# A hybrid decoder step on one core: state products in two tiles side by side, a minimum ahead of other work, another expert group kept on chip, and a closing stage with fewer VectorE products

## The chip, the cores and the metric

The kernel runs on one core of a Trainium2 chip. The metric is the device time of one execution in microseconds (us); lower is better. The engines of the core are called PE (TensorE), DVE (VectorE), ACT (ScalarE), POOL (GpSimd) and SP (SyncE, which here only issues DMAs). Each runs its own list of instructions in order and waits on semaphores.

## The reference, cut to what matters

One layer of a decoder, for 512 prompt tokens and 32 sample tokens (8 sequences of 4), `D_MODEL` 1024:

```
xn = rmsnorm(h); z, xbc, dt, gate, xl = split(xn @ w_in)
y_ssd = rmsnorm((ssd_chunked(conv(xbc), dt) + d_skip * xs) * silu(z))      # 16 heads of 64, state 64, chunks of 128
y_lru = rmsnorm(lru_scan(conv(xl)) * gelu(gate))
h = h + concat(y_ssd, y_lru) @ w_out
h = h + peer(rmsnorm(h))                    # 16384 experts of one neuron: act = gelu(t @ U), out = (gate * act) @ V
g = sigmoid(rmsnorm(h) @ w_ple_gate)
h = h + rmsnorm((p @ w_ple_proj) * g)
return rmsnorm(h), new states
```

For each of the 8 sample sequences the SSD part computes an output from the old state (`C . s0`) and a new state (`decay * s0 + B^T . (w * x)`). All is fp32.

## The kernel before, in words

Tensors lie feature-major: 8 blocks of 128 features on the partitions, 544 tokens along the free axis; the closing stage works on the two halves of 272 tokens (`q`). A precise product is made of three fp32r matmuls (high by high, high by low, low by high), so each weight block is first rounded on ScalarE (`Whi`, `Rh`) and its rest taken on VectorE (`Wlo`, `Rl`). The order on each engine is written out by hand, step by step in `n`; nothing is scheduled automatically.

**Mixer** (steps `n` 0 to 50, one weight tile of 48 matmuls each on TensorE). From step 35 on the tiles of the output projection are interleaved with the four chunks of the SSD scan. For chunk `c`, `l_min(c)` on VectorE limits the exponent (`L[c]`, 128x2048), `exps(c)` on ScalarE takes 16 exponentials of it, `scores(c)` on VectorE multiplies it by `CBm`; then `y_sum`, `state_in` (four products `xdt`, `xw`), `lru_add` (two additions over 544 tokens) and `lo` (the next `Wlo`). TensorE does `state`, `outputs`, `xs_tokens` and then its weight tile. After the chunks come the sample tokens: `sample_tokens` (turned to rows), `sample_outputs` (16 small products, and for each of 8 sequences a matmul of `CZ`, 128x64, with the old state `s0s`, 128x512, all added up in partitions 0 to 63 of one PSUM bank), `yoS` and `sample_turn` (turned back), `ssd_lo` (the low part `yl`), the sums of squares `sq8`, and from step 43 the last eight tiles with `sample_state(b)`: a matmul of `BTb`, 64x128, with `xwS`, 64x512, into bank 4 or 5.

**Experts.** 144 items through a ring of four slots (`Rw` by DMA, `Rh` ACT, `Rl` DVE): 16 query tiles, and 128 U blocks of 24 matmuls each over 384 tokens. Their activations go to memory (`acts`), gate values too (`gates`). Then 128 V items of 24 matmuls. V works in groups of four blocks: `load_a` brings the activations back to one of five buffers `Aq`, `load_g` two groups of gates to `Gq`, `h_full` (DVE) multiplies them, `h_hi` (ACT) rounds, `h_lo` (DVE) takes the rest, which the group's first item waits for. `VGRP` is the order of the groups; the last U group (31) is kept on chip and is third. The experts of the other 160 tokens go through POOL's gathers (`ug`, 512 KB each), with one VectorE operation per gathered row.

**Closing.** 16 gate products (`gate(i)`, half `i // 8`, block `i % 8`) on TensorE; DVE `scaled`, ACT `sigmoid`, DVE `gated`, ACT `gated_square`, DVE `square_add`; a total over features on TensorE, root on ACT, reciprocal on DVE; then `residual` (a gain and a factor, then the addition to `h`), squares of `h`, the last root, and `final` (gain and factor), from which SP stores `y` in 16 pieces.

Of the kernel before, what the change touches and what calls it, by code (L numbers as in the profile page):

```python
# [14 lines left out]
P = 128  # L15
# [28 lines left out]
VGRP = [0, 1] + list(range(PK // 4 - KEEP, PK // 4)) + list(range(2, PK // 4 - KEEP))  # L44
# [135 lines left out]
def mixer(nc, sh, ring, x, wm, par, head, w_rg, w_ig, conv_in, s0, lru0, ssd_p, ssd_s, conv_o, lru_o):  # L180
# [8 lines left out]
    def after(offset, size):  # L189
# [19 lines left out]
        ("segm", [64, NB], F32), ("smS", [64, 3, HG], F32), ("eS", [64, HG], F32), ("selJ", [NH, HG], F32),  # L209
# [26 lines left out]
        ("Ls", [64, HG, 32], F32), ("xdS", [64, HG * HD], F32), ("yoS", [64, HG * HD], F32),  # L236
# [6 lines left out]
    (xwS, ces), _ = plan(nc, LA + 16384, ("xwS", [64, HG * HD], F32), ("ces", [P, HG, 32], F32))  # L243
# [3 lines left out]
        ("stt", [P, HG * HD], F32), ("BTb", [64, NB, P], F32))  # L247
# [30 lines left out]
    def sync(sp):  # L278
# [21 lines left out]
        for n in range(2, NW):  # L300
# [11 lines left out]
            if n == 4:  # L312
                sp.wait_ge(S("const"), 28)
# [51 lines left out]
    def pool(g):  # L365
# [33 lines left out]
        g.wait_ge(k, 23)  # L399
# [8 lines left out]
        g.wait_ge(k, 28)  # L408
# [33 lines left out]
    def tensor(pe):  # L442
# [115 lines left out]
        def outputs(c):  # L558
            pe.wait_ge(S("scs"), c + 1)
            pe.wait_ge(S("xdw"), 4 * (c + 1))  # L560
            if c == 0:
                pe.wait_ge(S("cbm"), 2)
# [21 lines left out]
        def sample_tokens():  # L584
            pe.wait_ge(S("zc"), 5)
            pe.wait_ge(S("xdw"), 4 * NC)
            for jj in range(4):
                for g in range(NG):
                    m = pe.matmul(PS[0:64, 7, jj * P:(jj + 1) * P], XZ[:, 4 * g + jj, :], ident[:, :],
                                  start=(g == 0), stop=(g == NG - 1))  # L590
            m.then_inc(S("tr"), 1)

        def sample_outputs():
# [11 lines left out]
            for b in range(NB):  # L605
                m = pe.matmul(PS[0:64, 6, :].rearrange("p (j d) -> p j d", j=HG), CZ[:, b * 64:(b + 1) * 64],
                              s0s[:, :, b, :], start=(b == 0), stop=(b == NB - 1))
            m.then_inc(S("ymm"), 1)

        def sample_turn():  # L610
            pe.wait_ge(S("sad"), 1)
            for jj in range(4):
                m = pe.transpose(PS[:, 7, jj * 64:(jj + 1) * 64], yoS[:, jj * P:(jj + 1) * P], ident[0:64, 0:64])
            m.then_inc(S("ymm"), 1)

        def sample_state(b):
            pe.wait_ge(S("xdw"), 4 * NC + 2)
            pe.wait_ge(S("cbm"), 4)
# [3 lines left out]
            pe.matmul(PS[:, 4 + b % 2, :], BTb[:, b, :], xwS[:, :], start=True, stop=True).then_inc(S("stm"), 1)  # L622
# [59 lines left out]
    def scalar(a):  # L682
# [90 lines left out]
        for n in range(1, NW + 1):  # L773
# [50 lines left out]
            if n == 19:  # L824
# [7 lines left out]
                a.copy(smS[:, :, :], PS[0:64, 5, 0:3 * HG].rearrange("p (q j) -> p q j", q=3)).then_inc(S("tmv"), 1)  # L832
# [73 lines left out]
    def vector(v):  # L906
# [120 lines left out]
        def scores(c):  # L1027
            v.wait_ge(S("lexp"), c + 1)
            v.wait_ge(S("cbm"), 2)
# [113 lines left out]
        for n in range(1, NW + 1):  # L1143
# [10 lines left out]
            if n == 37:  # L1154
# [4 lines left out]
                state_in(1)  # L1159
            if n == 38:  # L1160
# [4 lines left out]
                state_in(2)  # L1165
            if n == 39:
# [9 lines left out]
            if n == 40:  # L1176
                v.wait_ge(S("tr"), 2 * NC + 1)
                src = PS[0:64, 7, :].rearrange("p (j d) -> p j d", j=HG)
                for dst, q in ((xdS, 1), (xwS, 2)):
                    v.tensor_tensor(dst[:, :].rearrange("p (j d) -> p j d", j=HG), src,  # L1180
                                    smS[:, q, :].unsqueeze(2).broadcast_to([64, HG, HD]), ALU.mult
# [10 lines left out]
            if n == 37:  # L1192
                l_min(2)
            if n == 38:
                l_min(3)
# [42 lines left out]
            if n == 8:  # L1238
# [3 lines left out]
                v.wait_ge(S("const"), 28)  # L1242
# [9 lines left out]
            if n == 10:  # L1252
# [3 lines left out]
                v.wait_ge(S("const"), 28)  # L1256
# [1306 lines left out]
```

## Time and profile before

| | |
|---|---|
| runs (3) | median 1787.02 us, 1786.6 to 1788.82 |
| the profiled execution | 1784.59 us |
| its span | 1782.6 us |
| PE busy | 1729.5 us, 97% |
| DVE busy | 1513.1 us, 85% |
| ACT busy | 836.7 us, 47% |
| POOL busy | 548.8 us, 31% |
| mean granted TensorE clock | 0.995 |

The span is what the profiler sees between first and last instruction; the 2 us beyond it belong to start and end. A matmul counts as busy until its modelled end, so neighbours overlap and PE's share is no measure of its efficiency. What counts is where an engine is idle and what ended that.

### The profile page before, as it was taken

Reading aid. Unit: us, or ns where it says so; the run is one execution under the profiler, and the core shown is the slowest. Engines: PE = TensorE matmul, PEld = TensorE weight load, DVE = VectorE, ACT = ScalarE, POOL = GpSimd, SP = SyncE. Lnnn points to the kernel's source line nnn. Section 1 sums busy time; section 2 is a strip of 40 time slices with the busy share of each in tenths; the row PEclk is TensorE's granted clock in tenths of the full one; section 3 lists DMA queues with packets and bytes.
Section 4 is the critical chain, followed back from the end, with each engine's and each line's share of the span. In section 5 each row is a group of like instructions: output and inputs, shape, how many; then the busy total and the mean of one; then the engine's idle time right before and its main releaser. Section 6 shows DMA issues by size and latency. Waiting matters only on the chain.

```text
span 1782.6 us, 29695 instructions
## 1 busy us (share of the span) xinstructions
PE 1729.5 (97%) x11346; PEld 1695.0 (95%) x11346; DVE 1513.1 (85%) x2744; ACT 836.7 (47%) x1206; POOL 548.8 (31%) x416
## 2 busy tenths in 40 slices
PE   7999997999999999999999999999999999999996
PEld 6999997889999999999999999999999999999995
DVE  7757998877678789999999999779888988899877
ACT  5556652443333233357777777423333323333163
POOL 3100220000000013345444444355555554556300
PEclk9999999999999999999999999999999999999998
DMA  4212342135335556789999999999999999999611
GB/s 161 92 64 80 136 143 101 65 133 186 117 130 171 176 169 232 264 309 352 380 362 368 344 355 379 397 389 398 396 396 397 396 398 397 396 394 388 226 60 51
DMA packets 164716, 461.12 MB, mean 259 GB/s; under 512 B 17152, under 2 KB 77632, under 8 KB 161888
## 3 DMA queue, kind: packets, MB, share of 16 engines
q1 hardware_dynamic: 118496, 291.43, 45.3%
q0 software_dynamic: 46080, 167.79, 25.1%
q8 instruction: 91, 1.49, 0.3%
q14 instruction: 49, 0.40, 0.1%
HBM read 404.61 MB, written 54.56 MB: 258 GB/s over the span
## 4 chain that ended last, share of the span: by engine, by line
PE 59%; DMA 21%; DVE 14%; ACT 3%; issue 3%; SPq 0%; POOL 0%; DVEq 0%; ACTq 0%
DMA Rw<-vn 16%; PE PS L478 12%; PE PS L1619 8%; PE PS L1620 8%; PE PS L1621 8%; PE PS L1602 5%; PE PS L1690 5%; DVE Rl L176 2%; PE PS L2251 2%; DMA ug<-vn,idxU 2%; PE PS L1632 2%; PE PS L1633 2%; PE PS L1634 2%; DVE ug L2040 1%; ACT Rh L171 1%
## 5 line engine op out<-in xcount | busy, mean ns | idle before, releaser
L171 ACT CAST Rh<-Rw 128x1024 fp32r<-128x1024 f32 x272 | 284.3, 1046 | 341.7 <-DMA Rw<-vn 299.7
L176 DVE TENSOR_TENSOR Rl<-Rw,Rh 128x1024 fp32r<-128x1024 f32 x272 | 332.6, 1223 | 101.6 <-ACT Rh L171 99.6
L1578 POOL DMA_INDIRECT ug<-un,idxU x160 | 240.5, 1503 | 524.6 <-DVE dots L2040 343.2
L1632 PE MATMUL PS<-Hh,Rh 128*128 128x384 f32 x1024 | 344.4, 336 | 8.1 <-DVE Hl L2032 4.7
L1619 PE MATMUL PS<-Xh,Rh 128*128 128x384 f32 x992 | 342.6, 345 | 3.8 <-DVE Rl L176 2.8
L1634 PE MATMUL PS<-Hh,Rl 128*128 128x384 f32 x1024 | 342.7, 335 | 0.0
L1633 PE MATMUL PS<-Hl,Rh 128*128 128x384 f32 x1024 | 342.7, 335 | 0.0
L1620 PE MATMUL PS<-Xl,Rh 128*128 128x384 f32 x992 | 334.2, 337 | 0.0
L1621 PE MATMUL PS<-Xh,Rl 128*128 128x384 f32 x992 | 333.3, 336 | 0.0
L1578 POOL DMA_INDIRECT ug<-vn,idxU x160 | 261.8, 1636 | 217.5 <-DVE yacc L2045 173.8
L1632 PEld LDWEIGHTS PS<-Hh,Rh 128*128 128x128 f32 x1024 | 192.7, 188 | 11.8 <-issue 6.5
L1633 PEld LDWEIGHTS PS<-Hl,Rh 128*128 128x128 f32 x1024 | 192.7, 188 | 0.0
L1634 PEld LDWEIGHTS PS<-Hh,Rl 128*128 128x128 f32 x1024 | 192.6, 188 | 0.0
L1619 PEld LDWEIGHTS PS<-Xh,Rh 128*128 128x128 f32 x992 | 186.6, 188 | 5.8 <-DVE Rl L176 4.6
L1620 PEld LDWEIGHTS PS<-Xl,Rh 128*128 128x128 f32 x992 | 186.6, 188 | 0.0
L1621 PEld LDWEIGHTS PS<-Xh,Rl 128*128 128x128 f32 x992 | 186.2, 188 | 0.0
L2045 DVE SCALAR_TENSOR_TENSOR yacc<-ug,coef,yacc 128x1024 f32<-128x1024 f32 x128 | 164.1, 1282 | 10.7 <-DMA ug<-vn,idxU 7.9
L1736 ACT ACTIVATE Ab<-PS 128x384 f32<-128x384 f32 x120 | 59.0, 491 | 238.8 <-PE PS L1621 235.9
L2040 DVE CUSTOM_DVE_ANT_0 ug<-ug,xtok 128x1024 f32<-128x1024 f32 x128 | 154.4, 1224 | 16.7 <-DMA ug<-un,idxU 16.2
L478 PE MATMUL PS<-xhi,Whi 128*128 128x272 f32 (+1 forms) x560 | 119.0, 294 | 9.9 <-DVE xlo L927 8.3
L478 PE MATMUL PS<-xhi,Wlo 128*128 128x272 f32 (+1 forms) x560 | 116.4, 289 | 0.0
L478 PE MATMUL PS<-xlo,Whi 128*128 128x272 f32 (+1 forms) x560 | 116.1, 289 | 0.0
(441 smaller groups left out, 3049.3 us busy)
## 6 DMA issues: line engine op xcount, KB each, us to landing
Rw<-uw SPq DMA_DIRECT2D x144, 512.0 KB
Rw<-vn SPq DMA_DIRECT2D x128, 512.0 KB
Wr<-wm SPq DMA_DIRECT2D x51, 512.0 KB, 3.3
gates<-stg SPq DMA_DIRECT2D x12, 2048.0 KB
acts<-Ab SPq DMA_DIRECT2D x124, 192.0 KB
Aq<-acts SPq DMA_DIRECT2D x31, 768.0 KB, 17.2
Gq<-gates SPq DMA_DIRECT2D x29, 768.0 KB
L<-acsd SPq DMA_DIRECT2D x4, 1024.0 KB, 7.2
```

The costliest lines, as they stand in the source:

```text
L171: a.copy(self.Rh[:, q, :], self.Rw[:, q, :]).then_inc(self.S("rhi"), 1)
L176: v.tensor_tensor(self.Rl[:, q, :], self.Rw[:, q, :], self.Rh[:, q, :].bitcast(F32), ALU.subtract).then_inc(self.S("rlo"), 1)
L478: r = pe.matmul(pair(b, m)[:, q, :], w_sb[:, s, k, 0:m], x_sb[:, k, q * HT:(q + 1) * HT], start=first, stop=last)
L1578: p.indirect_dma_start(out=ug[:, r % 4, :], out_offset=None, in_=un if r < IDC else vn, in_offset=bass.IndirectOffsetOnAxis(ap=idxU[:, r % ...
L1619: pe.matmul(out, Rh[:, q, w], x_hi[:, k, P:NP], start=(k == 0), stop=False)
L1620: pe.matmul(out, Rh[:, q, w], x_lo[:, k, P:NP], start=False, stop=False)
L1621: r = pe.matmul(out, Rl[:, q, w], x_hi[:, k, P:NP], start=False, stop=(k == ND - 1))
L1632: pe.matmul(out, Rh[:, q, w], hh, start=(g == 0), stop=False)
L1633: pe.matmul(out, Rh[:, q, w], hl, start=False, stop=False)
L1634: r = pe.matmul(out, Rl[:, q, w], hh, start=False, stop=(g == PK - 1))
L2040: v.tensor_tensor_reduce(ug[:, q, :], ug[:, q, :], (xtok if own else xtokS)[:, :], 1.0, 0.0, ALU.mult, ALU.add, dots[:, c:c + 1]).then_inc ...
L2045: v.scalar_tensor_tensor(out=y[:, :], in0=ug[:, q, :], scalar=coef[:, c:c + 1], in1=y[:, :], op0=ALU.mult, op1=ALU.add).then_inc(S("sdt"), 1)
```

## The change

What it does, part by part:

- **Mixer, tiles.** `sample_outputs` writes even sequences to partitions 0 to 63 and odd ones to 64 to 127 of the bank (two column tiles); `eS`, `yoS` and the other scalars have 128 partitions, and `sample_turn` adds the two halves by a product with `BZ`, which then holds the identity twice. `sample_state(b)` takes partitions 0 to 63 or 64 to 127 of `BTb` and `xwS` (two row tiles). To fill both halves, `token_scalars`, `sample_cb` and `sample_tokens` make their products twice, for each column half. POOL prepares four more small masks.
- **Mixer, order.** `l_min(2)` and `l_min(3)` stand directly behind `state_in` instead of behind `lru_add` and `lo`.
- **Experts.** `VGRP` is 0, 31, 1, 2, ...: the kept group is second. Group 1 is loaded five items into V instead of before it. `h_full(1)` and `h_hi(1)` come one and one item later.
- **Closing.** The gain of the residual and of the last norm is applied by ScalarE (`gain`, `final_gain`); VectorE multiplies and adds two blocks at a time (128x2x272), with plain two-operand products. The total of the first half, its reciprocal and its residuals come one gate earlier.

```diff
-VGRP = [0, 1] + list(range(PK // 4 - KEEP, PK // 4)) + list(range(2, PK // 4 - KEEP))
+VGRP = [0] + list(range(PK // 4 - KEEP, PK // 4)) + list(range(1, PK // 4 - KEEP))
...
             for jj in range(4):
                 for g in range(NG):
-                    m = pe.matmul(PS[0:64, 7, jj * P:(jj + 1) * P], XZ[:, 4 * g + jj, :], ident[:, :],
-                                  start=(g == 0), stop=(g == NG - 1))
+                    for u in range(2):
+                        m = pe.matmul(PS[64 * u:64 * u + 64, 7, jj * P:(jj + 1) * P], XZ[:, 4 * g + jj, :], ident[:, :],
+                                      start=(g == 0), stop=(g == NG - 1))
...
             for b in range(NB):
-                m = pe.matmul(PS[0:64, 6, :].rearrange("p (j d) -> p j d", j=HG), CZ[:, b * 64:(b + 1) * 64],
-                              s0s[:, :, b, :], start=(b == 0), stop=(b == NB - 1))
+                u = b % 2
+                m = pe.matmul(PS[64 * u:64 * u + 64, 6, :].rearrange("p (j d) -> p j d", j=HG),
+                              CZ[:, b * 64:(b + 1) * 64], s0s[:, :, b, :], start=(b < 2), stop=(b >= NB - 2))
...
-                m = pe.transpose(PS[:, 7, jj * 64:(jj + 1) * 64], yoS[:, jj * P:(jj + 1) * P], ident[0:64, 0:64])
+                m = pe.matmul(PS[:, 7, jj * 64:(jj + 1) * 64], yoS[:, jj * P:(jj + 1) * P], BZ[:, :],
+                              start=True, stop=True)
...
-            pe.matmul(PS[:, 4 + b % 2, :], BTb[:, b, :], xwS[:, :], start=True, stop=True).then_inc(S("stm"), 1)
+            r = slice(64 * (b % 2), 64 * (b % 2) + 64)
+            pe.matmul(PS[:, 4 + b % 2, :], BTb[r, b, :], xwS[r, :], start=True, stop=True).then_inc(S("stm"), 1)
...
                 state_in(1)
+                l_min(2)
...
-            if n == 37:
-                l_min(2)
...
-            if n == GEND:
+            g = m - VI
+            if g == 5:
                 sp.wait_ge(S("gmm"), NU)
-                load_a(1)
-            g = m - VI
+                load_a(2)
...
-        def residual(q, k):
-            v.scalar_tensor_tensor(out=half(mv[:, k, :], q), in0=half(mv[:, k, :], q), scalar=sh.col("norm_plo", k),
-                                   in1=rstdO[:, q, :], op0=ALU.mult, op1=ALU.mult).then_inc(S("csc"), 1)
-            v.wait_ge(S("csc"), q * ND + k + 1)
-            v.tensor_tensor(half(h[:, k, :], q), half(h[:, k, :], q), half(mv[:, k, :], q), ALU.add
-                            ).then_inc(S("res"), 1)
+        def residual(q, p):
+            v.wait_ge(S("csm"), q * ND + 2 * p + 2)
+            v.tensor_tensor(two(mv, q, p), two(mv, q, p), over_two(rstdO[:, q, :]), ALU.mult).then_inc(S("csc"), 1)
+            v.wait_ge(S("csc"), q * (ND // 2) + p + 1)
+            v.tensor_tensor(two(h, q, p), two(h, q, p), two(mv, q, p), ALU.add).then_inc(S("res"), 2)
```

The first place is VectorE in step 37 of the mixer, from the last product of `state_in(1)` to the exponent of chunk 2 (`L_159`); before:

```order
L1039 TENSOR_TENSOR xw<-PS,TM 128x512
L1087 TENSOR_TENSOR tmpL<-PS,rstdL 128x544 [waits ole,rst,mm]
L1089 TENSOR_TENSOR h<-h,tmpL 128x544 [waits ole]
L912 TENSOR_TENSOR Wlo<-Wr,Whi 128x1024 [waits whi]
L1016 TENSOR_TENSOR L_159<-L_159,TM 128x2048 [waits tmv,ab1]
L1053 TENSOR_TENSOR stt<-ST,dec 128x512 [waits stu,cem]
L1057 TENSOR_TENSOR ST<-stt,PS 128x512 [waits stm,stu]
L1061 COPY dec<-ce 128x8 [waits ce1]
L1063 TENSOR_TENSOR ce<-ce,xs 128x1024 [waits cem]
L1031 TENSOR_TENSOR L_159<-L_159,CBm 128x2048 [waits cbm,lexp]
```

and with the change:

```order
L1055 TENSOR_TENSOR xw<-PS,TM 128x512
L1032 TENSOR_TENSOR L_159<-L_159,TM 128x2048 [waits tmv,ab1]
L1103 TENSOR_TENSOR tmpL<-PS,rstdL 128x544 [waits ole,rst,mm]
L1105 TENSOR_TENSOR h<-h,tmpL 128x544 [waits ole]
L928 TENSOR_TENSOR Wlo<-Wr,Whi 128x1024 [waits whi]
L1069 TENSOR_TENSOR stt<-ST,dec 128x512 [waits stu,cem]
L1073 TENSOR_TENSOR ST<-stt,PS 128x512 [waits stm,stu]
L1077 COPY dec<-ce 128x8 [waits ce1]
L1079 TENSOR_TENSOR ce<-ce,xs 128x1024 [waits cem]
L1047 TENSOR_TENSOR L_159<-L_159,CBm 128x2048 [waits cbm,lexp]
```

The minimum moved ahead of two additions and one weight split; the product that waits for the exponentials (`lexp`) stands where it stood.

The second place is SP's queue around the last U items and the first V items (`Rw<-vn` is a V block into the ring); before:

```order
L164 DMA Rw<-vn 128x1024 [waits rlo,rhi]
L1505 DMA Aq_227<-acts 128x4x384 [waits as2,as1,as3,as0,gmm]
L164 DMA Rw<-vn 128x1024 [waits rlo,rhi] x3
L1514 DMA Gq_239<-gates 128x6x128 [waits gw1]
L1514 DMA Gq_239<-gates 128x6x128
L164 DMA Rw<-vn 128x1024 [waits rlo,rhi]
L1514 DMA Gq_239<-gates 128x6x128 x2
```

and with the change:

```order
L164 DMA Rw<-vn 128x1024 [waits rlo,rhi] x3
L1520 DMA Aq_228<-acts 128x4x384 [waits as2,as1,as3,as0,gmm]
L164 DMA Rw<-vn 128x1024 [waits rlo,rhi]
L1533 DMA Gq_239<-gates 128x6x256 [waits gw1]
L164 DMA Rw<-vn 128x1024 [waits rlo,rhi]
L1533 DMA Gq_239<-gates 128x6x256
```

The activations of the second V group are gone from here; those of the third are loaded two ring blocks further on. The gate pieces of 128 numbers now belong to `Gq_238`, earlier in the queue.

The third place is VectorE at the end, from the reciprocal of the second half's first norm on; before (eight pairs like the first two, of which six are left out at the dots):

```order
L2374 RECIPROCAL c_rstdO<-c_rstdO 128x272 [waits root]
L2399 SCALAR_TENSOR_TENSOR c_mv<-c_mv,par,c_rstdO 128x272 [waits rst]
L2402 TENSOR_TENSOR h<-h,c_mv 128x272 [waits csc]
L2399 SCALAR_TENSOR_TENSOR c_mv<-c_mv,par,c_rstdO 128x272
L2402 TENSOR_TENSOR h<-h,c_mv 128x272 [waits csc]
...
L2374 RECIPROCAL c_rstdF<-c_rstdF 128x272 [waits root]
L2408 SCALAR_TENSOR_TENSOR c_y<-h,par,c_rstdF 128x272 [waits rst]
L2408 SCALAR_TENSOR_TENSOR c_y<-h,par,c_rstdF 128x272 x7
```

and with the change (four pairs, two left out):

```order
L2416 RECIPROCAL c_rstdO<-c_rstdO 128x272 [waits root]
L2448 TENSOR_TENSOR c_mv<-c_mv,c_rstdO 128x2x272 [waits csm,rst]
L2450 TENSOR_TENSOR h<-h,c_mv 128x2x272 [waits csc]
L2448 TENSOR_TENSOR c_mv<-c_mv,c_rstdO 128x2x272 [waits csm]
L2450 TENSOR_TENSOR h<-h,c_mv 128x2x272 [waits csc]
...
L2416 RECIPROCAL c_rstdF<-c_rstdF 128x272 [waits root]
L2456 TENSOR_TENSOR c_y<-c_y,c_rstdF 128x2x272 [waits csm,rst]
L2456 TENSOR_TENSOR c_y<-c_y,c_rstdF 128x2x272 [waits csm] x3
```

Half as many operations stand there, each over two blocks, and they wait for ScalarE's gains (`csm`).

## Rows read from the trace of the kernel before

**Rows 1.** Windows: stretch, us, busy per engine, granted clock, DMA share, GB/s.

```profile
250.00:310.00 60.00, 48.97 (x502) 44.20 (x501) 52.10 (x79) 26.28 (x73) 0.52 (x2) 0.97 0.46 145
...
1131.00:1603.00 472.00, 464.00 (x2652) 460.52 (x2650) 408.33 (x344) 156.69 (x144) 244.10 (x153) 1.00 1.04 395
...
1743.00:1782.60 39.60, 22.32 (x132) 17.52 (x130) 33.65 (x68) 14.31 (x33) 0.00 (x0) 0.88 0.17 57
```

**Rows 2.** Timeline, VectorE, mixer: start, us, operation, [idle before <- who ended it].

```profile
273.36 2.28 DVE L1016 TENSOR_TENSOR L<-L,TM 128x2048 f32<-128x2048 f32 x1
...
280.49 2.29 DVE L1031 TENSOR_TENSOR L<-L,CBm 128x2048 f32<-128x2048 f32 x1 [2.18 <-ACT L L754]
...
296.83 2.29 DVE L1031 TENSOR_TENSOR L<-L,CBm 128x2048 f32<-128x2048 f32 x1 [2.19 <-ACT L L754]
...
319.71 0.72 DVE L1087 TENSOR_TENSOR tmpL<-PS,rstdL 128x544 f32<-128x544 f32 x1
320.46 0.73 DVE L1089 TENSOR_TENSOR h<-h,tmpL 128x544 f32<-128x544 f32 x1
321.10 1.22 DVE L912 TENSOR_TENSOR Wlo<-Wr,Whi 128x1024 fp32r<-128x1024 f32 x1
323.60 0.68 DVE L1329 TENSOR_TENSOR yoS<-PS,eS 64x512 f32<-64x512 f32 x1 [1.28 <-PE PS L606]
...
335.94 1.40 DVE L1113 SCALAR_TENSOR_TENSOR yl<-xs,par,yh 128x32 fp32r<-128x32 f32 x8 [2.25 <-ACT sq L886]
```

**Rows 3.** Timeline, ScalarE: the exponentials of chunk 2.

```profile
275.67 4.78 ACT L754 ACTIVATE L<-L,nacm 128x128 f32<-128x128 f32 x16 [10.61 <-DVE L L1016]
```

**Rows 4.** Timeline, TensorE, mixer: small products and where it waits.

```profile
220.31 1.16 PE L527 MATMUL PS<-xs 64*128 64x128 f32 x16
...
303.73 1.08 PE L554 MATMUL PS<-xw,Btok 128*64 128x512 f32 x4 [3.22 <-DVE xw L1039]
304.61 1.95 PE L571 MATMUL PS<-L,xdt 128*64 128x128 f32 x32
...
307.52 1.96 PE L589 MATMUL PS<-ident,XZ 128*64 128x128 f32 x16
...
316.48 7.08 PE L606 MATMUL PS<-s0s,CZ 128*64 128x512 f32 x16
...
344.71 1.15 PE L670 MATMUL PS<-sq,ones 128*128 128x272 f32 x4 [0.20 <-DVE sq L1358]
...
358.13 1.98 PE L622 MATMUL PS<-xwS,BTb 64*128 64x512 f32 x4
```

**Rows 5.** Windows, behind a wait of TensorE in the mixer.

```profile
278.00:281.00 3.00, 3.00 (x15) 3.00 (x14) 0.82 (x2) 3.00 (x10) 0.00 (x0) 0.50 0.59 178
```

**Rows 6.** Timelines, VectorE and TensorE, first V group.

```profile
1144.56 1.23 DVE L2040 CUSTOM_DVE_ANT_0 ug<-ug,xtok 128x1024 f32<-128x1024 f32 x1 [1.75 <-DMA ug<-un,idxU]
...
1151.61 1.76 DVE L2025 TENSOR_TENSOR Aq<-Aq,Gq 128x1536 f32<-128x1536 f32 x1 [3.01 <-DMA Aq<-acts]
...
1148.75 0.66 PE L1632 MATMUL PS<-Hh,Rh 128*128 128x384 f32 x1 [3.04 <-DVE Hl L2032]
```

**Rows 7.** Chain of waits: start, us, what; two gate products of the closing.

```profile
1737.12 6.03 PE PS L2251 x48
```

**Rows 8.** Timelines, VectorE and then SP, end of the closing.

```profile
1743.17 0.44 DVE L2381 TENSOR_TENSOR c_tmp<-PS,c_rstdG 128x272 f32<-128x272 f32 x1 [1.27 <-PE PS L2251]
...
1756.39 0.43 DVE L2381 TENSOR_TENSOR c_tmp<-PS,c_rstdG 128x272 f32<-128x272 f32 x1
...
1760.39 1.85 DVE L2374 RECIPROCAL c_rstdO<-c_rstdO 128x272 f32<-128x272 f32 x1 [1.36 <-ACT c_rstdO L2306]
...
1769.39 1.84 DVE L2374 RECIPROCAL c_rstdF<-c_rstdF 128x272 f32<-128x272 f32 x1
...
1776.46 3.39 DVE L2408 SCALAR_TENSOR_TENSOR c_y<-h,par,c_rstdF 128x272 f32<-128x272 f32 x8
...
1776.99 3.79 SPq L2214 DMA_DIRECT2D y<-c_y  x8
```

More of the change, by code:

```diff
@@ L1165, in vector @@
                 state_in(2)
+                l_min(3)
             if n == 39:
@@ L1435, in experts @@
     GRP = 4 * 4 * DT
-    a_at = [R0 + 8 * GRP, R0, R0 + 2 * GRP, R0 + 7 * GRP, ring.end]
+    a_at = [R0 + 8 * GRP, R0 + 2 * GRP, R0, R0 + 7 * GRP, ring.end]
     Aq = [nc.alloc_sbuf_tensor_at("Aq%d" % q, [P, 4, DT], F32, offset=o) for q, o in enumerate(a_at)]
@@ L2101, in vector @@
                 h_lo(g // 4 + 1)
-            if g >= -2 and g % 4 == 2 and g // 4 + 2 < PK // 4:
+            if g == -1:
+                h_full(1)
+            if g >= 2 and g % 4 == 2 and g // 4 + 2 < PK // 4:
                 h_full(g // 4 + 2)
@@ L2302, in gated_square, with gain, final_gain @@
             a.activation(sq[:, i % 4, :], half(mv[:, n, :], q), ACT.Square).then_inc(S("csq"), 1)
+        def gain(i):
+            q, n = i // ND, i % ND
+            a.wait_ge(S("csq"), ND + i + 1)
+            a.activation(half(mv[:, n, :], q), half(mv[:, n, :], q), ACT.Copy, scale=sh.col("norm_plo", n)
+                         ).then_inc(S("csm"), 1)
+        def final_gain(q, k):
+            a.wait_ge(S("res"), q * ND + k + 1)
+            a.activation(half(yb[:, k, :], q), half(h[:, k, :], q), ACT.Copy, scale=sh.col("norm_fin", k)
+                         ).then_inc(S("csm"), 1)
         def root(buf, src, count):
@@ L2354, in scalar @@
                 a.preload_act_table(ACT.Sigmoid)
-            if i >= 12:
-                for k in range(2 * (i - 12), 2 * (i - 12) + 2):
+            elif i >= 1:
+                gated_square(i - 1)
+                gain(i - 1)
+            if i >= 11 and i < 15:
+                for k in range(2 * (i - 11), 2 * (i - 11) + 2):
                     res_square(0, k)
@@ L2360, in scalar @@
         root(rstdO[:, 1, :], PS[:, 7, 0:HT], 8)
+        gain(2 * ND - 1)
         root(rstdF[:, 0, :], PS[:, 6, 0:HT], 11)
         for k in range(ND):
-            res_square(1, k)
+            final_gain(0, k)
+            if k % 2 == 1 and k >= 3:
+                res_square(1, k - 3)
+                res_square(1, k - 2)
+        res_square(1, ND - 2)
+        res_square(1, ND - 1)
         root(rstdF[:, 1, :], PS[:, 7, 0:HT], 11 + ND)
+        for k in range(ND):
+            final_gain(1, k)
     def vector(v):
@@ L2446, in vector @@
         recip(rstdO[:, 1, :], 7)
-        for k in range(ND):
-            residual(1, k)
+        for p in range(ND // 2):
+            residual(1, p)
         final(0)
```

142 lines of the change are left out of this document (81 added, 61 removed).

## The prediction

> **What bounds the kernel now.** I read the windows first, to find stretches in which TensorE is idle, then the timelines of the engine it waits for. Over the 472 us from 1131 on TensorE is busy for 464.0; between 250 and 310 us it is busy for 49.0 of 60, and from 1743 on for 22.3 of 39.6 [rows 1]. So three places have something to give, and they are the three that the change touches; elsewhere only TensorE's own work counts.
>
> *Mixer, 250 to 310.* VectorE is the pacemaker. It waits twice for ScalarE's exponentials, 2.18 and 2.19 us [rows 2], and ScalarE in turn had been idle for 10.61 us before them because the minimum came so late [rows 3]. TensorE waits 3.22 us for VectorE's `xw` [rows 4]. From 310 to 345 TensorE has no gap, but it is only just covered: at 344.71 it still waits 0.20 us for the sums of squares, the end of a VectorE and ScalarE chain that begins at `yoS`, 323.60 [rows 2, 4]. Whatever TensorE saves in between is worth no more than that chain gains.
>
> *First V group.* TensorE waits 3.04 us for `Hl`; shortly before VectorE had waited 1.75 us for a gathered row, and behind `Hl` it waits 3.01 us for the activations of group 1 [rows 6]. But the DMA engines run at a share of 1.04 and 395 GB/s over the whole of 1131 to 1603 [rows 1].
>
> *Closing, from 1743.* VectorE. Two gate products take 6.03 us on TensorE [rows 7], 3.01 each. The eleventh gate's factor followed its product at once (1743.17, after a wait of 1.27), so the last one, four gates on, could have been at 1755.2; it stands at 1756.39 [rows 8]. Then follow the reciprocal at 1760.39, residuals to 1769.39, and two finals.
>
> **Mixer, order of the minimum.** `l_min` is put ahead of two additions and a split. From start to start these take 0.75 (319.71 to 320.46), 0.64 (to 321.10) and about 1.14 us [rows 2], 2.5 together, more than each wait. ScalarE was idle, so both waits go: 2.18 + 2.19 = **4.4 us**. What is late in exchange: the two additions and `Wlo`, by the 2.28 us of the minimum [rows 2]. `Wlo` is for the next weight tile, ahead of which TensorE does the state products and sits in its 11 us of idle time [rows 1]; cover enough. If that cover were gone it would cost up to 2.28 per step.
>
> **Mixer, column tiles.** `sample_outputs` takes 7.08 us for 8 products of 128x64 with 128x512 [rows 4]. `state` is the same shape, with its two products already in the two column halves: the next operation starts 0.88 us after them (303.73 to 304.61) [rows 4]. So 8 products come to 4 x 0.88 = 3.5 us, 3.5 less. Of these only a part reaches the chain: `yoS` waited for TensorE, but before that VectorE was busy with a split until 1.28 us earlier [rows 2], so `yoS` can move by 1.3 beyond the 4.4. The chain gains 4.4 + 1.3 = **5.7 us** at 344.71. It has no slack I can see elsewhere: TensorE's wait of 0.20 says that TensorE, which gains 4.4 + 3.5 = 7.9, will arrive early and wait about 2 us, at the first tile that needs `yl` (335.94) or at 344.71.
>
> The doubled products for the other half: `sample_tokens` has 16 records in 1.96 us and gets 32, alternating between the halves; `outputs` does 32 of the same 128 moving columns, alternating, in 1.95 [rows 4]. So nothing is added. The Trainium skill ("TensorE: Matmul & The Clock Gate", "Part 3: Packing small matmuls — row/col tiling") says that a weight load overlaps running products only when its row group differs; column tiles share their row group. By that rule the doubling would show in full, 1.96 us on the chain, and the sum below would be 9.8 instead of 11.8. The row of `outputs` speaks against it, and I go by the row.
>
> **Mixer, row tiles.** `sample_state`: two products take 1.98 us one after the other [rows 4]. The trace has no 512-column product in two row tiles. Bounds: nothing gained, or the 0.88 to 1.08 us of the column pair, 0.9 to 1.0 gained. The nearest row is `cb`, 16 records of 64x128 with 128 columns, alternating rows, in 1.16 us, 0.07 each, against 0.12 each for the 16 records of `sample_tokens` in one tile [rows 4]: row tiles do run side by side. I take 0.95 for each of four pairs. The first pair stands before the wait at 344.71 and is hidden in it; three count: **2.9 us**. After 350 nothing but TensorE's own work sets the pace there.
>
> **Mixer, additions.** Three tiny products in `token_scalars`, one in `sample_cb`, four longer ones in `sample_turn`: by the 0.07 to 0.12 us of small records [rows 4] some **0.3 us**; `BZ` on VectorE (64 columns) 0.15 us, in front of a wait for ScalarE; POOL's masks at the start, needed by no one for 20 us. Mixer in all: 5.7 + 2.9 - 0.3 = **8.3 us**. The U phase behind it is paced by TensorE, so this passes through.
>
> **Experts.** The load of 768 KB goes from before V to behind its start. VectorE's 3.01 us for it go; the gathered row probably comes earlier, and TensorE's 3.04 could shrink by the 1.75 that VectorE lost to it [rows 6]. But no byte is saved. With the DMA engines full until 1603 [rows 1], data for a V item arrive when the bytes ahead of it have passed, whoever waits at the start; TensorE idles 472 - 464.0 = 8.0 us there, 3.04 at the start and 5.0 later. Less at the start means more later. I take **0**; bounds: a gain of 3.0 if it is kept, a loss of 1.5 if the pieces of 128 numbers, now ahead of `h_full(0)`, come late. The new load of group 2 has some 15 us until its use.
>
> **Closing.** Earlier reciprocal and pairwise residuals: each pair of blocks took four operations; now two, at the rate of the 544-token additions (0.75 + 0.64 = 1.39) [rows 2]. The last factor is then no longer behind TensorE: 1756.39 - 1755.2 = 1.2; between it and the root ScalarE has one gain (some 0.35) in place of two squares: 0.25. Residuals, 1760.39 to 1769.39, are a reciprocal (1.88) and 7.1 us; four times 1.39 is 5.6: 1.5 less. The first final: from 1769.39 to the second one's first product at 1776.46 are two reciprocals and eight products of 0.41 (3.39 for eight) [rows 8]; four of 0.64 save 0.7. Its first product covers two blocks, 0.72 instead of 0.50: 0.2 lost. That is 1.2 + 0.25 + 1.5 + 0.7 - 0.2 = 3.45. Behind it stands SP: it starts at 1776.99, when the first product is done, and needs 3.79 us for eight stores, more than the 3.39 of VectorE [rows 8]. So the end is set by when the first `c_y` of the second half is ready, and VectorE's shorter last products give nothing more: **3.5 us**. ScalarE gets 32 more short operations; it is busy for less than half of each gate.
>
> **Sum.** 8.3 + 0 + 3.5 = 11.8 us. The profiled execution of 1784.59 becomes 1772.8; it lies 2.4 below the median of the runs, 1787.02, which becomes **1775.2 us**, 0.66% less. A difference of 0.2%, 3.6 us, is about what a measurement of this kernel can tell from none.
>
> **Rivals.**
> 1. *The gain at the start of V is kept.* For it: VectorE's wait of 3.01 blocks the ring and the gathers behind it. Against it: full DMA engines. 1.5 to 3 us more: 1772.2 to 1773.7. Chance 0.2.
> 2. *The tiles don't overlap* (the change doesn't do what it says). `sample_outputs` and `sample_state` stay as long, and `sample_tokens` costs 1.96 more. The chain then gains 4.4 - 2.0 = 2.4 and nothing follows; less 0.3: 2.1, with the closing 5.6: 1781.4. Against it the rows of `state` and `outputs`. Chance 0.08.
> 3. *The closing gives nothing*, because ScalarE, with gains between squares, becomes late there: 8.3 us: 1778.7. Against it its idle time. Chance 0.08.
> 4. *Slower.* One mechanism: TensorE's clock. After a wait in the mixer it was granted at 0.50, 1.2 GHz, for 278 to 281, in which 15 records ran [rows 5]. The change makes new waits of about 2 us between 328 and 345. At half clock work takes twice its time, so every microsecond of full-speed work costs one more. To end above no change by 3.6 it must last for over 11.8 + 3.6 = 15.4 us of such work, two and a half weight tiles; with five tiles, 30 us, it would be 1805. For it: that the drop happened at all; against: it lasted 3 us. Chance 0.04.
>
> The forecast has 0.55; the rest is spread around it. For the range: below, rival 1 with a quicker end, 1770.8; above, rival 2, 1781.5. The forecast's own range is 1773.5 to 1777. Faster by over 0.2%: 0.9; within: 0.06; slower: 0.04.
>
> **What would show it.** In the trace after: no wait of VectorE for exponentials in `scores(2)` and `scores(3)`; 16 records of `sample_outputs` in 3.5 us; a wait of TensorE of about 2 us between 325 and 340; pairs of `sample_state` in about 1.0; a first V product that waits less, and more waits later, with the stretch from its first to its last product some 1.5 to 3 us longer between waits; the last reciprocal about 3.5 nearer to the last gate; stores still 0.47 apart. It would be wrong if TensorE's wait in the mixer were 4 us or more, if a wait for `ole` or `wlo` appeared at steps 38 or 39, or if V ended earlier than the start's gain taken back.

## The result, and the profile after

The changed kernel takes 1776.18 us (median of 4 runs, 1774.02 to 1777.85) against 1786.94 (4 runs): ratio 0.994, 95% interval 0.9924 to 0.9955. The forecast was 1775.2. The profiled execution after is the fastest of the four, 1774.02 us with a span of 1772.0; against 1784.59 and 1782.6 before that is 10.6 us less, where the sum had said 11.8. By three marks, the first expert product (398.20 before, 391.60 after), the first closing product (1693.19 and 1685.59) and the end of the span, the 10.6 divide into **6.6 in the mixer, 1.0 in the experts, 3.0 in the closing**; the sum had 8.3, 0 and 3.5. The errors partly cancel.

**Mixer.** VectorE's timeline of the changed kernel (start, us, operation, [idle before <- who ended it]); it answers to [rows 2]:

```profile
271.16 2.28 DVE L1032 TENSOR_TENSOR L<-L,TM 128x2048 f32<-128x2048 f32 x1
278.56 2.29 DVE L1047 TENSOR_TENSOR L<-L,CBm 128x2048 f32<-128x2048 f32 x1
...
292.62 2.29 DVE L1047 TENSOR_TENSOR L<-L,CBm 128x2048 f32<-128x2048 f32 x1
...
318.04 0.68 DVE L1344 TENSOR_TENSOR yoS<-PS,eS 128x512 f32<-128x512 f32 x1
...
341.75 3.55 DVE L1120 RECIPROCAL rstdB<-rstdB 128x544 f32<-128x544 f32 x1 [0.80 <-ACT rstdB L765]
...
346.81 4.42 DVE L1387 TENSOR_TENSOR s0s<-s0s,ces 128x4096 f32<-128x4096 f32 x1
```

Both products with `CBm` stand without a wait, and `yoS` starts without one, 5.56 us earlier than before. TensorE's timeline of the same kernel, to be read beside [rows 4]:

```profile
299.51 1.08 PE L565 MATMUL PS<-xw,Btok 128*64 128x512 f32 x4 [0.93 <-DVE xw L1055]
...
303.30 1.97 PE L601 MATMUL PS<-ident,XZ 128*64 128x128 f32 x32
...
312.25 3.65 PE L619 MATMUL PS<-s0s,CZ 128*64 128x512 f32 x16
...
321.96 1.00 PE L627 MATMUL PS<-BZ,yoS 128*128 128x64 f32 x8
...
330.78 0.49 PE L486 MATMUL PS<-yh,Whi 128*128 128x272 f32 x2 [1.76 <-DVE yl L1129]
...
333.05 0.66 PE L486 MATMUL PS<-yh,Whi 128*128 128x272 f32 x2
...
338.49 1.13 PE L638 MATMUL PS<-xwS,BTb 64*128 64x512 f32 x4
339.55 1.18 PE L686 MATMUL PS<-sq,ones 128*128 128x272 f32 x4
...
347.04 0.49 PE L486 MATMUL PS<-yh,Whi 128*128 128x272 f32 x2 [0.30 <-DVE h L1116]
...
353.23 1.13 PE L638 MATMUL PS<-xwS,BTb 64*128 64x512 f32 x4
...
355.23 0.49 PE L486 MATMUL PS<-yh,Whi 128*128 128x272 f32 x2 [0.87 <-DVE h L1116]
```

The eight products with the old state take 3.65 instead of 7.08, the doubled `sample_tokens` 1.97 for twice the records, a pair of `sample_state` 1.13 instead of 1.98. The new wait of 1.76 stands where it was expected. Behind it a group of two records takes 0.66 instead of the usual 0.41: here the clock was granted at its lower level. Not expected were the waits for `h` at 347 and 355: TensorE wants a PSUM pair which VectorE has not yet added to `h`. At 355 VectorE is late because of the 4.42 us product on `s0s`. The wait of 0.30 at 347 has another cause: that product starts only at 346.81, behind the addition which ends the wait. Run e8, the same mixer at full clock, has the wait of 0.87 (at 354.58) and not the one of 0.30, and its reciprocal of `rstdB` starts at 341.11 instead of 341.75; so the 0.30 goes with the half clock.

**Experts.** All of TensorE's waits at V items of the changed kernel:

```profile
1141.38 0.41 PE L1647 MATMUL PS<-Hh,Rh 128*128 128x384 f32 x1 [2.29 <-DVE Hl L2049]
...
1312.85 0.44 PE L1647 MATMUL PS<-Hh,Rh 128*128 128x384 f32 x1 [0.57 <-DVE Rl L176]
...
1326.97 0.41 PE L1647 MATMUL PS<-Hh,Rh 128*128 128x384 f32 x1 [1.34 <-DVE Hl L2049]
...
1458.32 0.44 PE L1647 MATMUL PS<-Hh,Rh 128*128 128x384 f32 x1 [1.73 <-DVE Rl L176]
...
1463.80 0.41 PE L1647 MATMUL PS<-Hh,Rh 128*128 128x384 f32 x1 [1.02 <-DVE Hl L2049]
...
1477.32 0.44 PE L1647 MATMUL PS<-Hh,Rh 128*128 128x384 f32 x1 [0.79 <-DVE Rl L176]
...
1549.52 0.41 PE L1647 MATMUL PS<-Hh,Rh 128*128 128x384 f32 x1 [1.18 <-DVE Hl L2049]
```

The first wait is 0.75 smaller than in [rows 6]; the six behind it come to 6.63 us, where the kernel before had eight with 4.93. ScalarE's timeline shows what is behind the one at 1458, a ring block that arrived late, and VectorE's what is behind the one at 1326.97, a gathered row that arrived late:

```profile
1455.96 1.05 ACT L171 CAST Rh<-Rw 128x1024 fp32r<-128x1024 f32 x1 [7.52 <-DMA Rw<-vn]
```

```profile
1322.73 1.28 DVE L2062 SCALAR_TENSOR_TENSOR yacc<-ug,coef,yacc 128x1024 f32<-128x1024 f32 x1 [1.02 <-DMA ug<-vn,idxU]
```

The other four go back to a DMA in the same way: those at 1312 and 1477 to ring blocks that ScalarE waited 6.93 and 8.07 us for, that at 1463 to the block at 1455.96, behind which VectorE has no gap, and that at 1549 to a row that VectorE waited 0.91 us for.

**Closing.** VectorE and SP of the changed kernel from the last factor on, beside [rows 8]:

```profile
1747.49 0.44 DVE L2423 TENSOR_TENSOR c_tmp<-PS,c_rstdG 128x272 f32<-128x272 f32 x1 [1.27 <-PE PS L2270]
...
1751.42 1.85 DVE L2416 RECIPROCAL c_rstdO<-c_rstdO 128x272 f32<-128x272 f32 x1 [1.36 <-ACT c_rstdO L2336]
1753.31 0.72 DVE L2448 TENSOR_TENSOR c_mv<-c_mv,c_rstdO 128x544 f32<-128x544 f32 x1
1754.14 0.73 DVE L2450 TENSOR_TENSOR h<-h,c_mv 128x544 f32<-128x544 f32 x1
1754.78 0.72 DVE L2448 TENSOR_TENSOR c_mv<-c_mv,c_rstdO 128x544 f32<-128x544 f32 x1
...
1759.18 1.84 DVE L2416 RECIPROCAL c_rstdF<-c_rstdF 128x272 f32<-128x272 f32 x1
...
1765.60 2.63 DVE L2456 TENSOR_TENSOR c_y<-c_y,c_rstdF 128x544 f32<-128x544 f32 x4
```

```profile
1761.87 8.28 SPq L2233 DMA_DIRECT2D y<-c_y  x16
```

The last factor now waits for TensorE, as forecast. A pair of residuals takes 1.47 us from start to start (1753.31 to 1754.78): the addition follows its product after 0.83, not after the 0.75 that the sum took over from the mixer.

### The profile page after: what moved, and what is told of

It is laid out like the page before. It is cut to its first block and busy times, and to the rows that moved or that the text cites. A ratio compares the mean times of both kernels' runs of the same rounds, so it can differ in the third digit from the quotient of the medians.

```text
span 1772.0 us, 29786 instructions
## 1 busy us (share of the span) xinstructions
PE 1721.9 (97%) x11375; PEld 1693.5 (96%) x11375; DVE 1508.3 (85%) x2722; ACT 849.9 (48%) x1238; POOL 561.5 (32%) x420
## 5 line engine op out<-in xcount | busy, mean ns | idle before, releaser
L1593 POOL DMA_INDIRECT ug<-vn,idxU x160 | 271.7, 1698 | 207.8 <-DVE yacc L2062 164.5
```

The costliest lines, as they stand in the source:

```text
L1593: p.indirect_dma_start(out=ug[:, r % 4, :], out_offset=None, in_=un if r < IDC else vn, in_offset=bass.IndirectOffsetOnAxis(ap=idxU[:, r % ...
```

## The experiments

Each time is set against the kernel before, measured beside it (medians 1786.47 us for e1 to e4, 1787.29 for e5 to e8, 1786.67 for e9 to e11, 1785.96 for e12). A ratio is followed by its 95% interval; 0.001 is 1.8 us. "Stretch" is the time from the first V product to the first closing product in the trace.

**The parts, first four runs.** The order of the minimum alone:

```diff
                 state_in(1)
+                l_min(2)
...
-            if n == 37:
-                l_min(2)
```

> The kernel before with l_min(2) and l_min(3) behind state_in and nothing else of the change. My theory: VectorE's two waits for exponentials (2.18 and 2.19 us) go and its whole chain up to the sums of squares moves by them: 4.4 us less than the kernel before, the mixer ends 4.4 earlier. Rival: the additions and the weight split that the minimum now stands ahead of are late instead, and TensorE or the chain waits for them: the traces would show a wait for ole or wlo, and 0 to 2 us gained.

1781.98 us, ratio 0.9973 (0.9964 to 0.9982): 4.5 less by the medians, 4.8 by the ratio. In the trace the mixer ends 4.5 earlier (393.70 against 398.20), with no wait for `ole` or `wlo`. My theory holds. But its first V product, at 1143.45, is 5.3 earlier than before and its first closing product, 1690.91, only 2.3: the stretch is 3.0 longer, with 8.2 us of waits in it. By the medians the whole gain arrived, so the stretch differs from one execution to the next: with the same V stage it took 544.4 us in the kernel before, 547.5 here and 543.4 in e3.

The V order undone, with its loads, `h_full` and `h_hi`; of the edit only the order is shown:

```diff
-VGRP = [0] + list(range(PK // 4 - KEEP, PK // 4)) + list(range(1, PK // 4 - KEEP))
+VGRP = [0, 1] + list(range(PK // 4 - KEEP, PK // 4)) + list(range(2, PK // 4 - KEEP))
```

> The changed kernel with the V order, the loads of groups 1 and 2 and h_full and h_hi of group 1 as before. Theory that V gives the start's gain back (DMA engines full): within 1 us of the changed kernel, so 9.8 to 10.8 less than the kernel before; the two traces give 1.0 for this part, of which 1.4 is the TensorE clock that fell behind the wait of 3.04 us and did not behind 2.29. Rival, the start's gain is kept: this kernel loses the 3.0 us, 7.8 less than the kernel before.

1776.01 us, 0.9941 (0.9928 to 0.9955): as fast as the changed kernel. The part is worth nothing that can be told. The rival's 7.8 us less, a ratio of 0.9956, lies just outside the interval. So the 1.0 us between the two profiled executions can't be credited to the edit.

The closing alone:

> The kernel before with the closing stage of the change alone. By my forecast 3.5 us less than before; by the two traces, from the last V product to the end, 3.0 less. Rival, ScalarE with its gains becomes late in the closing: 0.

1782.97 us, 0.9982 (0.9973 to 0.9992), 3.5 less by the medians, 3.2 by the ratio; the rival's 0 is outside the interval. Its trace has 86.4 us from the first closing product (1693.80) to the end of the span (1780.2) against 89.4 before: 3.0.

The tiles undone:

```diff
-                m = pe.matmul(PS[64 * u:64 * u + 64, 6, :].rearrange("p (j d) -> p j d", j=HG),
-                              CZ[:, b * 64:(b + 1) * 64], s0s[:, :, b, :], start=(b < 2), stop=(b >= NB - 2))
+                m = pe.matmul(PS[0:64, 6, :].rearrange("p (j d) -> p j d", j=HG), CZ[:, b * 64:(b + 1) * 64],
+                              s0s[:, :, b, :], start=(b == 0), stop=(b == NB - 1))
...
-            pe.matmul(PS[:, 4 + b % 2, :], BTb[r, b, :], xwS[r, :], start=True, stop=True).then_inc(S("stm"), 1)
+            pe.matmul(PS[:, 4 + b % 2, :], BTb[:, b, :], xwS[:, :], start=True, stop=True).then_inc(S("stm"), 1)
```

> The changed kernel with all sample products in one tile as before; order of the minimum, V group and closing as changed. By my forecast the tiles are worth 1.3 on the chain, 2.9 in sample_state, less 0.3: 3.9, so 7 us less than the kernel before. By the traces the mixer gained 6.6, of which the order should be 4.4, so the tiles 2.2: 8.6 less than before. Rival, tiles worth nothing: 10.8 less.

1776.47 us, 0.9948 (0.9934 to 0.9961). By the time alone the tiles can't be told from nothing. The trace can tell: its mixer ends at 393.73, 2.1 later than the changed kernel's 391.60. So the tiles gave 2.1 in that execution, not 3.9. The next runs show where the rest is.

**Where the rest of the tiles' gain is: VectorE.**

```diff
             if n == 42:
...
+                v.wait_ge(S("abs"), 64)
+                s0_decay(0)
                 for k in range(ND):
                     ssd_lo(k, 1)
```

`s0_decay(0)` is the first half of the 4.42 us product; the second stays behind `ssd_add`.

> The changed kernel with half of the old states' decay (one product of 4.42 us on VectorE) moved into VectorE's wait of 2.25 us ahead of the second part of yl. Theory: TensorE's new waits of 0.30 at 347 and 0.87 at 355 come from VectorE's late additions behind that product; they go, and the mixer ends 1.2 us earlier, about 12 less than before. Rival, the row tiles gain nothing whatever VectorE does: no change.

1774.35 us, 0.9929 (0.9916 to 0.9943). VectorE's timeline of this run:

```profile
329.03 2.28 DVE L1037 TENSOR_TENSOR s0s<-s0s,ces 128x2048 f32<-128x2048 f32 x1
331.36 1.39 DVE L1134 SCALAR_TENSOR_TENSOR yl<-xs,par,yh 128x32 fp32r<-128x32 f32 x8
...
347.12 2.28 DVE L1037 TENSOR_TENSOR s0s<-s0s,ces 128x2048 f32<-128x2048 f32 x1
```

The half fills the gap of 2.25 and delays `yl` by nothing, and TensorE's waits at 347 and 355 are gone. Executions reach this place up to 1.7 us apart, so the mixer is measured from the `outputs` of chunk 0: from there to the first expert product it is 127.82 us (263.16 to 390.98) against 128.75 in run e8 (262.20 to 390.95), whose mixer is that of the changed kernel at full clock. The same mixer took 128.74 to 128.76 in e5, e9 and e10 as well. So the wait for `h` at 355 cost 0.9, shown in the trace; in the time the gain is within the uncertainty. Without the tiles the mixer takes 131.79 (e1 and e4). At full clock the tiles are thus worth 3.0, and with VectorE's delay removed 4.0, close to the forecast's 3.9.

```diff
+            if n == OS0:
+                sample_state(0)
+                sample_state(1)
             tile(n)
```

> The edit of the run before, and sample_state(0) and (1) ahead of the weight tile that waits for yl, so that their 1.1 us lie in TensorE's wait of 1.76. Theory: the wait shrinks to 0.7, the clock does not fall behind it, and TensorE reaches the sums of squares before VectorE has them; 0.4 us less than the run before, 12.4 less than the kernel before. Rival, the half clock is hidden by the wait for the sums anyway: 0.

1775.07 us, 0.9931 (0.9918 to 0.9945), no less than e6. The wait for `yl` is 0.69, and TensorE then waits 2.11 for the sums instead of 1.04; from chunk 0 to the first expert product it is again 127.82. What TensorE saves ahead of the sums is waited out there, as the rival says. This pair of runs tests the wait alone: in e6's profiled execution the clock did not fall behind its wait of 1.76 either. The half clock does cost something where it occurs: from `outputs` of chunk 0 the changed kernel needs 129.44 (262.16 to 391.60) and e2 129.42, 0.7 more than the same mixer in e8, where the records behind the wait ran at full clock.

**Why V gives back.** The V items want a ring block (512 KB) each 4.17 us, 126 GB/s; activations and gates, 47 each; and 1.40 gathered rows of 512 KB, 176: some 396 GB/s in all. That sum is an estimate and leaves out three single loads that fall into the stretch (`wp_raw`, `ple_raw`, `cw_raw`, 2.1 MB together, 4.6 GB/s over 459 us), so some 401 GB/s are wanted. The windows of the changed kernel (stretch, us, busy per engine, clock, DMA share, GB/s) show 396 moved:

```profile
1131.00:1590.00 459.00, 450.08 (x2585) 447.35 (x2584) 397.21 (x332) 151.89 (x140) 252.41 (x150) 1.00 1.04 396
```

The single loads also fall together. SP issues them between 1417 and 1460, and is held for 8.41 us by the largest:

```profile
1432.29 8.41 SPq L2194 DMA_DIRECT2D wp_raw<-w_plp  x1
```

Between 1440 and 1485 TensorE waits 2.7 to 4.3 us in each of the ten traces without moved rows, 3.54 of the 6.63 us in the changed kernel. e5 and e10 have the same loads at this place and no wait, so the loads alone don't make the waits; whether moving them would also remove these was not tried.

Two runs move rows out of the crowded stretch:

```diff
-    ROWS = [(46, 0), (78, 36), (VI - 1, 146), (NALL - 5, 2 * IDC)]
+    ROWS = [(46, 0), (78, 36), (VI - 1, 146), (VI + 103, 283), (NALL - 5, 2 * IDC)]
```

> The changed kernel with 9 of the expert rows taken later: V items up to 103 use 137 rows instead of 146, the last 20 use 37 instead of 28. The bytes up to 1600 fall from about 397 GB/s wanted (a ring block each 4.17 us, 126; activations and gates, 47 each; 1.40 rows of 512 KB, 176) to 386. Theory that V's waits come from DMA engines at their limit of 395 to 397 GB/s: most of the 6.6 us of waits behind the first product go and the kernel is 3 to 6 us faster than the changed one, 14 to 17 less than before. Rival, the waits come from how the loads bunch together, not from their sum: no more than 1 us.

1773.18 us, 0.9923 (0.9909 to 0.9936), 3 less than the changed kernel; the time alone does not exclude the rival's 1, the trace speaks for the theory. TensorE has no wait between the first V product and 1600; but with 1.85 rows an item behind that, VectorE is overloaded: from 1608 to 1676 TensorE is busy for 64.1 of 68 us, all 68 in the changed kernel, and one of the waits is this:

```profile
1626.15 0.41 PE L1647 MATMUL PS<-Hh,Rh 128*128 128x384 f32 x1 [0.88 <-DVE Hl L2049]
```

```diff
-    ROWS = [(46, 0), (78, 36), (VI - 1, 146), (NALL - 5, 2 * IDC)]
+    ROWS = [(42, 0), (78, 41), (VI - 1, 151), (VI + 103, 290), (NALL - 5, 2 * IDC)]
```

> The changed kernel with 5 expert rows taken earlier, in the U stage, and 2 later than V item 103: items up to there use 1.34 rows instead of 1.40, so 389 GB/s are wanted instead of 397, and the last 20 use 1.5, so that VectorE is not overloaded there as it was with 1.85. Theory: no waits of TensorE in V before 1600 as in the run with rows late, and none behind it: 4 to 5 us less than the changed kernel. Rival: the added rows make VectorE late in the U stage, and the gain is lost there.

**1769.35 us**, 0.9899 (0.9884 to 0.9915): 7 less than the changed kernel, more than expected. TensorE's waits between 1131 and 1600, first in the changed kernel, then here:

```profile
PE PS L1647 <- DVE Hl L2049: 5.8, 4, 2.3
PE PS L1647 <- DVE Rl L176: 3.1, 3, 1.7
```

```profile
PE PS L1647 <- DVE Hl L2049: 2.0, 1, 2.0
```

One wait is left, the first. The rows wanted in the crowded stretch are 5% fewer, 1.34 an item instead of 1.40, and all bytes 2% fewer: with the three single loads some 394 GB/s instead of 401. By this estimate the demand stood just above what the engines deliver and now stands just below; the windows show 396 here too, so the estimate is some 2 short. TensorE is now busy for 457.0 of the 459 us:

```profile
1131.00:1590.00 459.00, 457.00 (x2627) 456.71 (x2626) 399.85 (x328) 155.22 (x142) 235.41 (x145) 1.00 1.04 396
```

The theory holds for V. A moved row also takes 1.28 us of VectorE's work along, and no run moves the one without the other. But VectorE is no less busy in the stretch than before (399.9 us, 397.2 in the changed kernel), while its waits for gathered rows of V fall from 10.5 to 3.4 us: the trace speaks for the DMA engines.

The rival, a loss in the U stage, is partly true. From 840 to 1130 TensorE is busy without a gap, but the loss lies ahead of that. TensorE in the changed kernel, then here:

```profile
733.29 0.44 PE L1634 MATMUL PS<-Xh,Rh 128*128 128x384 f32 x1 [1.37 <-DVE Rl L176]
```

```profile
734.24 0.45 PE L1634 MATMUL PS<-Xh,Rh 128*128 128x384 f32 x1 [2.38 <-DVE Rl L176]
```

VectorE's timeline shows a second gathered row ahead of the ring block's low part, where the changed kernel has one:

```profile
730.68 1.22 DVE L2057 CUSTOM_DVE_ANT_0 ug<-ug,xtok 128x1024 f32<-128x1024 f32 x1
...
731.82 1.22 DVE L2057 CUSTOM_DVE_ANT_0 ug<-ug,xtok 128x1024 f32<-128x1024 f32 x1
...
732.97 1.22 DVE L176 TENSOR_TENSOR Rl<-Rw,Rh 128x1024 fp32r<-128x1024 f32 x1
```

This wait is 2.38 in all three runs with the moved rows (e10, e11, e12) and 1.35 to 1.37 in the eleven other traces. From the first expert product to the last U product it takes 748.8 us here and 747.2 in the changed kernel. Of these 1.6 only the 1.0 can be put down to the edit: e8, without moved rows, shows 748.8 too, by a wait of 1.51 at 784. From the last U product to the first closing product it is 539.1 instead of 546.8.

**Is a gain at the start of V kept?**

```diff
-            if n == GEND + 3:
-                h_lo(0)
...
             for r in rows(n):
+                if n == GEND + 2 and r == rows(n)[1]:
+                    h_lo(0)
```

> The changed kernel with h_lo(0) ahead of a gathered row and a ring block's low part instead of behind them. In the trace of the changed kernel Hh of the first group is ready at 1136.6, TensorE's last U product ends at 1139.1, and Hl was made at 1139.5 only; so TensorE's wait of 2.3 us at the first V product goes. Theory that V gives a gain at its start back while the DMA engines are full: waits behind it grow, from the last U product to the last V product no more than 1 us is gained, and the time stays within 1 us of the changed kernel. Rival, it is kept: 2.3 us less than the changed kernel, 3.8 where the clock fell behind the wait.

1775.17 us, 0.9932 (0.9918 to 0.9945). TensorE's timeline of this run, at the first V product and behind it:

```profile
1139.48 0.44 PE L1647 MATMUL PS<-Hh,Rh 128*128 128x384 f32 x1 [0.58 <-ACT Aq L1747]
...
1169.07 0.45 PE L1647 MATMUL PS<-Hh,Rh 128*128 128x384 f32 x1 [0.18 <-DVE Rl L176]
1178.63 0.45 PE L1647 MATMUL PS<-Hh,Rh 128*128 128x384 f32 x1 [0.97 <-DVE Rl L176]
```

The first product is 1.9 earlier than in the changed kernel, and from 1169 on ring blocks are missing. From the last U product to the first closing product it takes 548.4 us (1138.56 to 1686.98), in the changed kernel 546.8 (1138.75 to 1685.59), and 546.9 to 550.1 in the eight other traces without moved rows: nothing is to be seen of the 1.7 us less of waiting at the start. The trace speaks against the rival. The time doesn't exclude it: 2.3 less than the changed kernel would be a ratio of about 0.993, inside the interval.

> The changed kernel with the mild shift of rows, h_lo(0) early, half of the old states' decay early, and stores of two blocks. If each part is kept when the DMA engines have room: 4.5 for the rows, 2.3 to 3.8 at the start of V, 0.9 in the mixer, 1.3 at the end: 9 to 10.5 less than the changed kernel, 20 less than before. If the start of V is given back even with room: 6.7 less than the changed kernel.

1767.24 us, 0.9885 (0.9867 to 0.9903), 19.4 less than before and about 9 below the changed kernel, of which the rows are 7, the decay 0.9 and the stores 0.6 (e8 below). The 9 fall into the range that was stated for a kept start only because the rows gave 7 and not the 4.5 put in for them. Its first V product waits 0.58 and the clock stays up behind it, but the ring makes TensorE wait 1.38 at 1172. The last run takes `h_lo(0)` back:

> The run before with h_lo(0) back in its old place: rows shifted mildly, half of the decay early, stores of two blocks. In the run before, the first V product waited 0.58 instead of 2.0, but TensorE waited 1.38 for a ring block at 1172 and the stretch from the last U product to the first closing product was 1.3 us longer than with the rows alone. Theory, the gain at the start of V is given back even with 389 GB/s wanted: within 1 us of the run before. Rival, it is kept and the wait at 1172 was chance: 1.5 us or more slower than the run before.

1767.06 us, 0.9897 (0.988 to 0.9914): the same median. The ratios to the kernel before differ by 0.0012, 2 us, with intervals of 3 us either way, so the times don't decide. The traces do, as far as single executions can. The first V product of this run waits 1.92 and the clock falls behind it, which costs 1.6 more. Yet from the last U product (1139.27) to the first closing one (1678.76) it takes 539.5 us, against 540.3 in the run before (1140.50 to 1680.80) and 539.1 in e10. So the start of V is given back even with 2% fewer bytes wanted. A guess at the reason, not tried: the engines come into V with a backlog, since the last 290 us of the U stage move 366 GB/s at a DMA share of 0.98.

**Stores.**

```diff
-            for k in range(ND):
-                sp.wait_ge(S("yd"), q * ND + k + 1)
-                sp.dma_start(half(y[:, k, :], q), half(yb[:, k, :], q)).then_inc(S("y_out"), 16)
+            for p in range(ND // 2):
+                r = slice(2 * p, 2 * p + 2)
+                sp.wait_ge(S("yd"), q * ND + 2 * p + 2)
+                sp.dma_start(y[:, r, q * HT:(q + 1) * HT], yb[:, r, q * HT:(q + 1) * HT]).then_inc(S("y_out"), 16)
```

> The changed kernel with y stored in 8 DMAs of two blocks instead of 16 of one. Theory that SP's pace of 0.47 us a store sets the end: the last store leaves when the last product is done, at about 1768.3 instead of 1770.1 on the trace's time: 1.3 us less, 12 less than before. Rival, the larger store takes as much longer to land: 0.

1774.71 us, 0.993 (0.9916 to 0.9943). In the trace the end of the span is 5.8 us behind the start of the last final (1766.90 to 1772.7), in the changed kernel 6.4 (1765.60 to 1772.0): 0.6 gained, not 1.3. SP's pace is half of the story; what else lies in the 5.8 these runs don't settle.

## Why the prediction was right, point by point

- **Order of the minimum, 4.4.** Right: 4.5 in the trace of e1 and 4.5 to 4.8 in its time. What was made late, two additions and `Wlo`, made nobody wait.
- **Column tiles, 3.5 in TensorE and 1.3 on the chain.** Right in both: 3.43 (7.08 to 3.65), and `yoS` stands at 318.04, 1.1 earlier than without tiles (e4, 319.16) although that execution began 0.2 sooner. The doubled `sample_tokens` costs nothing, 32 records in 1.97 against 16 in 1.96. By the rule of the Trainium skill ("TensorE: Matmul & The Clock Gate", "Part 3: Packing small matmuls — row/col tiling") it would have cost another 1.96; the measurement decides against that reading of it.
- **Row tiles, 2.9.** A pair took 1.13 (1.98 before), 0.85 less each and not 0.95: 2.6 for three. The step that failed is "After 350 nothing but TensorE's own work sets the pace there". It was read from a trace in which TensorE did not wait there. VectorE's product of 4.42 us on `s0s` stands ahead of the additions that free PSUM; once the tiles had put TensorE ahead it waited 0.87 for one of them. e6 took this out by moving half of that product and got 0.9 back. Column tiles 1.3, row tiles 2.6, less 0.9, are the 3.0 that the tiles gave at full clock.
- **Clock.** Named as a rival that would have to last 15 us to decide. It fell behind the wait of 1.76 at 330.78 and stayed down for some 4 us. The sums cover most of it; 0.7 came through, here and in e2. The sum had nothing for it.
- **Additions, 0.3.** Of that size: the offset of the changed kernel at `outputs` of chunk 0 is 0.3 (262.16 against 261.82), though executions differ by more. `sample_turn` took 1.00 instead of 0.46.
- **Experts, 0.** Right in the time: e2 equals the changed kernel. The mechanism has two halves. That the waits go when fewer bytes are wanted is shown by e5 and e10. That a gain at the start is waited out at the ring rests on the single traces of e9, e11 and e12. One sign that the prediction named did not come: the stretch from the first to the last V product should have been 1.5 to 3 us longer; up to the first closing product it was 544.2 us, before 544.4. Between the two profiled executions the part came to 1.0. In the kernel before the clock fell behind the wait of 3.04 (the first product took 0.66, not 0.41) and cost 1.4, but the stretch varies by more than that, so it is luck that the 1.0 makes up for part of what the mixer missed.
- **Closing, 3.5.** Mechanism right, the sum 0.5 too high, mostly by two terms. The factor moved by 1.3 (1.2 foreseen), the first final gained 0.65 (0.7) and the longer first product lost 0.26 (0.2). The residuals gained 1.24 instead of 1.5, since a dependent addition starts 0.83 and not 0.75 behind its product, and "0.25" for ScalarE's order was 0.07: the gap from the last factor to the reciprocal is 3.93, before 4.00.

Together: 8.3 + 0 + 3.5 foreseen, 6.6 + 1.0 + 3.0 found. The rival of tiles that don't overlap is refuted by the rows, "the closing gives nothing" by e3; a kept start is barely outside e2's interval and is spoken against by the traces of e9 and e12.

## What to carry to other kernels

A saving on one engine is worth what the engine behind it can follow: look not only for waits in the trace, but for the slack of the next thing needed, here a PSUM pair freed by VectorE. Where a stage's DMA demand, added up from its schedule with the single loads, stands at or above the rate that the windows show, an earlier start in it did not pay here; taking bytes out of the stretch did, and here 5% fewer gathered rows gave about 7 us, beside the 11 of the whole change. Look at where the moved work lands, too: one more gathered row ahead of a ring block on VectorE cost 1.0 us in the U stage. Time such edits over several executions: the same V stage took from 543.4 to 547.5 us.

## What the runs showed of the hardware

- Column tiles in alternation cost no more than one tile: 32 records of 128x64 weights and 128 moving columns in 1.97 us, 16 in 1.96; with 512 columns 0.46 per product instead of 0.88. Two row tiles of 64x128 weights and 512 columns take 1.13 a pair instead of 1.98.
- The clock does not follow the length of a wait alone. Behind the first V product's wait it fell to its lower level in e12 (1.92 us waited), in e10 (2.00 us waited, 1.6 us lost by the products behind it), in e5 (2.37) and in the kernel before (3.04), and not in the changed kernel (2.29) or e2 (2.80). Behind the wait for `yl` in the mixer it fell in the changed kernel and e2 (1.76 both), and not in e6 (1.76) or e8 (1.74).
- From 1131 to 1590 the windows show 396 GB/s at a DMA share of 1.04 in the changed kernel and in e10 alike: the rate stays, and TensorE's waits are there or not. e10 gets more items done in it, each with fewer bytes.
